# Attention by pairs of heads, and the last layer's expert weights read in rows of 2 and 4 KB

## The chip, the core and the metric

The program runs on one NeuronCore of one Trainium2 chip. TensorE (PE) multiplies matrices into PSUM, VectorE (DVE) and ScalarE (ACT) work on PSUM and SBUF, GpSimd (POOL) copies rows and issues indirect DMAs, and SyncE (SP) issues the transfers of the weights. The metric is the device time of one execution, in microseconds. All numbers are float32; the profile shows each float32 matmul as two PE records, and a transpose as one.

## The reference, cut to what matters

A first block of two layers is followed by a second block of one layer. In the second block the 8 attention heads of width 64 share 2 groups of keys and values, over 512 tokens. Three branches are gated per head and added:

```python
s_cmp = einsum('bghsd,bgcd->bghsc', qh, k_cmp) * scale                  # 31 compressed keys
p_cmp = softmax(where(cmp_mask, s_cmp, -1e30)) * cmp_mask
o_cmp = einsum('bghsc,bgcd->bghsd', p_cmp, v_cmp)
# N_SEL = 16 blocks of 64 cover all 512 tokens: the selected branch is causal attention
s = einsum('bghqd,bgqnld->bghqnl', qb, kg) * scale;  p = softmax(where(ok, s, -1e30))
o_slc = einsum('bghqnl,bgqnld->bghqd', p, vg)
# window 512: the window branch is causal attention with its own keys and values
o_win = einsum('bghnqk,bgnkd->bghnqd', softmax(where(ok_w, s_w, -1e30)), vwb)
o = gates[..., 0:1] * o_cmp + gates[..., 1:2] * o_slc + gates[..., 2:3] * o_win
...
top_i = top_k(where(emask, choice, -inf), 8)[1]        # 8 of 64 experts for each token
swiglu(t_pad[rb], w_gu[e], w_dn[e])                    # w_gu (1024, 512), w_dn (256, 1024)
```

## The kernel before, in words

The program is a list of stages with barriers between them, and each engine's instructions stand in the order in which they are written. Three stages matter.

**Rope** (`rope_stage`, profile from 3691 to 3712 us) rotates queries and keys. Beside it POOL clears `vpad` and copies the values of both causal branches into it (L2228, L2232), each head group's 64 columns with 64 zero columns on either side.

**Attention** (`attention_stage`) takes 96 units: head pair `c2` (4), block `t` of 128 queries (4), head `h` of the pair (2), branch `b` (3: selected, window, compressed). For a unit PE multiplies queries by keys with 64 contraction rows (L2300; L2295 for the compressed branch), adds a mask through the identity (L2302, L2297), later transposes the probabilities in blocks of 128 (L2312) and multiplies by the values (L2329, L2325), whose zero columns put head 0 in PSUM partitions 0 to 63 and head 1 in 64 to 127. DVE takes the maximum (L2348), scales it (L2352), inverts the sum (L2354) and scales the probabilities (L2361). ACT does the exponential with its sum (L2390) and moves the transposed block to SBUF (L2374). PE's order for unit u is scores(u), turn(u-1), values(u-2); DVE finishes unit u before it begins u+1. Score banks are three, banks of transposes two.

**The last layer's experts** (`sparse_experts_stage` with G = 2) hold 64 experts in 32 groups of two. A group's weights are three tiles of 2 MB: gate and up of each expert, and both down matrices. They lie in one of two sets, three slots of the weight ring or `moe_spare`. SP waits until the group before has freed a set (L1362), and before each tile until the tile two before it has landed (L1369), then issues it (L1370). Work goes in units of 64 rows, at least one for each expert, 97 in the profiled execution: POOL copies the gathered rows (L1401) and gathers again (L1386, an indirect DMA of 4 KB rows), PE transposes them (L1415), multiplies gate (L1427) and up (L1429) into PSUM partitions 0 to 63 and 64 to 127, ACT does silu (L1488), DVE the product (L1510), PE a transpose (L1437) and the down product (L1446), DVE copies it out (L1513), and ACT writes it to HBM in two DMAs of 64 rows by 2 KB (L1497). Three waits set the pace of these writes:

```python
act.wait_ge(s.y_copied, u + 2)
act.wait_ge(s.y_out, 32 * u + 64)     # ACT, before it sends unit u: the writes of unit u-1 have landed
...
dve.wait_ge(s.y_out, 32 * u + 32)     # DVE, before it copies unit u: those of unit u-2 have landed
```

Each weight tile lies packed in HBM: a partition's 16 KB are one row. The two layers of the first block use the same function with G = 1.

Of the kernel before, what the change touches and what calls it, by code (L numbers as in the profile page):

```python
# [10 lines left out]
ALU = mybir.AluOpType  # L11
# [5 lines left out]
P = 128  # L17
D = 1024
KD = D // P
T = 512  # L20
# [1298 lines left out]
def sparse_experts_stage(m, tag, first, groups, G, F, hidden, rows, r, source, after):  # L1319
# [25 lines left out]

    with st.block() as block:
        @block.sync
        def _(sp):
            ring.stream(sp, first + 3)
            for j in range(3):  # L1350
                sp.dma_start(bufs[1][j], source(1, j)).then_inc(spare_in[j], 16)
            with sp.Fori(1, halves) as i:
                for half in range(2):
# [3 lines left out]
                    for j in range(3):  # L1357
# [12 lines left out]
                        sp.dma_start(bufs[half][j], source(2 * i + half, j)  # L1370
# [846 lines left out]
def rope_stage(m, p):  # L2217
# [7 lines left out]
    with st.block() as block:  # L2225
        @block.gpsimd
        def _(pool):
# [6 lines left out]
            pool.wait_ge(s.vals, 2 * NT)  # L2234

# [32 lines left out]
def attention_stage(m, p, mT):  # L2268

    nc = m.nc
    st = Stage(m, "attn")
    NB = 3
    pr = st.sb("probs", [P, NB, T])
    pT = st.sb("probsT", [P, 2, NT, P])
    c = st.sb("cols", [P, NB, 4])
    s = st.sem("score top ntop exp total scaled turned t_moved out o_moved masked")

    units = [(c2, t, h, b) for c2 in range(4) for t in range(NT) for h in range(2) for b in range(3)]  # L2280

    def width(u):
        return NC if units[u][3] == 2 else (units[u][1] + 1) * P

    with st.block() as block:
        @block.tensor
        def _(pe):
            def scores(u):
                c2, t, h, b = units[u]
                g, rows, w = c2 // 2, slice(64 * h, 64 * h + 64), width(u)  # L2290
                if u >= 3:
                    pe.wait_ge(s.exp, u - 2)
                ps = m.ps[:, u % 3, :]
                if b == 2:
                    nc.tensor.matmul(ps[:, 0:NC], p.nq[rows, c2, t * P:(t + 1) * P], p.kcmp[rows, g, :],  # L2295
                                     start=True, stop=False)
                    last = nc.tensor.matmul(ps[:, 0:NC], m.ident, mask(p, "cneg")[:, t * NC:(t + 1) * NC],  # L2297
                                            start=False, stop=True)
                else:
                    nc.tensor.matmul(ps[:, 0:w], p.qr[rows, c2, t * P:(t + 1) * P], p.kr[rows, b, g, 0:w],  # L2300
                                     start=True, stop=False)
                    last = nc.tensor.matmul(ps[:, w - P:w], m.ident, mask(p, "causal"), start=False, stop=True)  # L2302
                last.then_inc(s.score, 1)

            def turn(u):
                w = width(u)
# [3 lines left out]
                for j in range(0, w, P):  # L2310
                    n = min(P, w - j)
                    last = nc.tensor.transpose(m.ps[0:n, 3 + u % 2, j:j + P], pr[:, u % NB, j:j + n], m.ident)  # L2312
                last.then_inc(s.turned, 1)

            def values(u):
                c2, t, h, b = units[u]
                g, o = c2 // 2, u // 6
                pe.wait_ge(s.t_moved, u + 1)
                first, final = u % 6 == 0, u % 6 == 5
                if first and o >= 2:  # L2320
                    pe.wait_ge(s.o_moved, o - 1)
# [12 lines left out]
            for u in range(n + 2):  # L2334
                if u < n:
                    scores(u)
                if 1 <= u <= n:
                    turn(u - 1)
# [356 lines left out]
```

## Time and profile before

| | us |
|---|---|
| time before, median of 3 (lowest, highest) | 5263.54 (5261.21, 5282.5) |
| the profiled execution: its own time | 5280.28 |
| its span in the profile | 5278.5 |
| mean granted PE clock, share of full speed | 0.842 |
| attention stage | 3713 to 4001 |
| the last layer's expert stage | 4275 to 5184 |

The page gives, for each engine, the time in which it was busy; the sharing of the span among stages is read from windows. A granted clock of 1.0 is 2.4 GHz and 0.5 is 1.2 GHz. "issue" in a wait means that nothing in the profile is shown as the releaser.

### The profile page before, as it was taken

To read this page: it belongs to the slowest core of one execution; us is meant where nothing else is said; L and a number is where in the kernel's file an instruction comes from. 1 tells how busy PE (TensorE), PEld (TensorE's weight loads), DVE (VectorE), ACT (ScalarE), POOL (GpSimd) and SP (SyncE) were. 2 spreads that over 40 slices of the span, in tenths; PEclk is the share of its full clock that TensorE was granted. 3 is DMA by queue.
4 is the path that set the end of the run, shared out by engine and by line. 5 is a ranking of instruction groups with operands and counts; after the bars stand their busy time and mean duration, and the time that the engine had idled before them with its cause. 6 is when DMAs were issued, how large, how long until landed. Compare 5 with 4: busy or idle time off the path is not lost. (4 is left out here: it accounts for less than half of the span.)

```text
span 5278.5 us, 55308 instructions
## 1 busy us (share of the span) xinstructions
PE 3959.5 (75%) x18979; PEld 2326.6 (44%) x18980; DVE 1353.0 (26%) x2466; ACT 776.8 (15%) x1604; POOL 895.4 (17%) x933
## 2 busy tenths in 40 slices
PE   7699998998387766984888578765998447777772
PEld 3368867983233322433333233323664224444441
DVE  0343453341300012122000120354433301111115
ACT  0232242220011110001111101100221001111110
POOL 0014413430111110001111100321000032222223
PEclk9799999898599988996999889876557679999986
DMA  6470000001399996123999852101001047676685
GB/s 242 121 185 1 1 32 17 1 2 64 115 405 406 386 372 228 48 84 148 393 391 411 337 219 75 54 0 52 7 1 46 33 171 281 248 278 244 252 301 172
DMA packets 144431, 900.30 MB, mean 171 GB/s; under 512 B 52963, under 2 KB 53861, under 8 KB 97829
## 3 DMA queue, kind: packets, MB, share of 16 engines
q1 hardware_dynamic: 95684, 805.05, 40.3%
q0 software_dynamic: 22368, 50.39, 3.0%
q10 hardware_dynamic: 26240, 43.01, 2.5%
q8 instruction: 87, 1.43, 0.1%
q14 instruction: 52, 0.42, 0.0%
HBM read 839.32 MB, written 78.46 MB: 174 GB/s over the span
## 5 line engine op out<-in xcount | busy, mean ns | idle before, releaser
L1427 PE MATMUL ps<-weight_ring,moe_xT 128*64 128x256 f32 (+1 forms) x1344 | 450.1, 490 | 77.9 <-issue 75.7
L1427 PE MATMUL ps<-moe_spare,moe_xT 128*64 128x256 f32 (+1 forms) x1280 | 425.5, 487 | 59.3 <-issue 59.2
L1429 PE MATMUL ps<-weight_ring,moe_xT 128*64 128x256 f32 (+1 forms) x1344 | 450.8, 491 | 0.0
L1429 PE MATMUL ps<-moe_spare,moe_xT 128*64 128x256 f32 (+1 forms) x1280 | 426.2, 488 | 0.0
L1401 POOL COPY moe_xg<-moe_xin 64x1024 f32<-64x1024 f32 x168 | 173.5, 1033 | 1430.5 <-PE ps L1415 802.3
L258 PE MATMUL ps<-weight_ring,mod_wide 128*128 128x512 f32 x640 | 290.7, 609 | 141.8 <-DVE mod_wide L241 132.6
L1510 DVE TENSOR_TENSOR moe_act<-moe_sg,ps 64x256 f32<-64x256 f32 (+1 forms) x164 | 87.2, 532 | 1090.2 <-ACT moe_sg L1488 1090.2
L1427 PEld LDWEIGHTS ps<-weight_ring,moe_xT 128*64 128x64 f32 x1344 | 190.8, 144 | 316.7 <-issue 284.4
L1427 PEld LDWEIGHTS ps<-moe_spare,moe_xT 128*64 128x64 f32 x1280 | 180.3, 143 | 285.8 <-issue 256.3
L1513 DVE COPY moe_y<-ps 128x512 f32 x164 | 113.4, 691 | 714.4 <-PE ps L1446 577.0
L1446 PE MATMUL ps<-weight_ring,moe_aT 128*64 128x512 f32 x944 | 256.5, 680 | 15.7 <-issue 15.6
L1446 PE MATMUL ps<-moe_spare,moe_aT 128*64 128x512 f32 x904 | 248.4, 687 | 14.3 <-issue 14.3
L258 PEld LDWEIGHTS ps<-weight_ring,mod_wide 128*128 128x128 f32 x640 | 121.4, 194 | 310.0 <-issue 176.0
L1437 PE MATMUL ps<-base,moe_act 64*128 64x64 f32 x462 | 61.7, 239 | 249.4 <-DVE moe_act L1510 249.4
L1312 POOL DMA_INDIRECT slot_table<-disp_ids,moe_dest x48 | 47.0, 979 | 1080.5 <-DVE moe_dest L1297 1067.1
L1488 ACT ACTIVATE moe_sg<-ps 64x256 f32<-64x256 f32 (+1 forms) x164 | 75.8, 462 | 1019.0 <-PE ps L1429 674.5
L1429 PEld LDWEIGHTS ps<-weight_ring,moe_xT 128*64 128x64 f32 x1344 | 190.6, 144 | 0.0
L1386 POOL DMA_INDIRECT moe_xin<-hidden,moe_icol x174 | 166.1, 955 | 137.3 <-POOL moe_icol L1382 135.7
L1415 PE MATMUL ps<-base,moe_xg 64*128 64x64 f32 x1336 | 151.2, 237 | 47.1 <-POOL moe_xg L1401 47.1
L1429 PEld LDWEIGHTS ps<-moe_spare,moe_xT 128*64 128x64 f32 x1280 | 180.3, 143 | 0.0
L1720 PE MATMUL ps<-hT,weight_ring 128*128 128x512 f32 x384 | 168.9, 603 | 9.9 <-DMA weight_ring<-in_w_in_b_dram 8.0
L527 PE MATMUL ps<-delta_hx,weight_ring 128*128 128x512 f32 x384 | 171.7, 602 | 5.6 <-PEq L184 5.6
(508 smaller groups left out, 6254.4 us busy)
## 6 DMA issues: line engine op xcount, KB each, us to landing
weight_ring<-in_w_dram SPq DMA_DIRECT2D x96, 2048.0 KB, 10.8
moe_spare<-in_w_dram SPq DMA_DIRECT2D x96, 2048.0 KB, 10.7
weight_ring<-in_w_exp_gu_dram SPq DMA_DIRECT2D x32, 2048.0 KB, 9.8
moe_spare<-in_w_exp_gu_dram SPq DMA_DIRECT2D x32, 2048.0 KB, 14.7
weight_ring<-in_ada_w_dram SPq DMA_DIRECT2D x24, 2048.0 KB, 8.1
expert_rows<-moe_y ACTq DMA_DIRECT2D x328, 128.0 KB
weight_ring<-in_w_exp_dn_dram SPq DMA_DIRECT2D x16, 2048.0 KB, 11.6
moe_spare<-in_w_exp_dn_dram SPq DMA_DIRECT2D x16, 2048.0 KB, 11.2
```

The costliest lines, as they stand in the source:

```text
L258: last = nc.tensor.matmul(m.ps[:, u % 4, :], wide[:, v, k, :], w[:, k, :], start=(k == 0), stop=(k == KD - 1))
L527: last = nc.tensor.matmul(m.ps[:, b, :], w[:, k, h * P:(h + 1) * P], hx[:, k, CT:CT + T], start=(k == 0), stop=(k == KD - 1))
L1386: nc.gpsimd.indirect_dma_start(out=xin[:, b, :], out_offset=None, in_=hidden, in_offset=bass.IndirectOffsetOnAxis(ap=icol[:, b:b + 1], axi ...
L1401: nc.gpsimd.tensor_copy(xg[:], xin[:, b, :]).then_inc(s.x_moved, 1)
L1415: last = nc.tensor.transpose(m.ps[:, 2, k * UR:(k + 1) * UR], xg[:, k * P:(k + 1) * P], m.ident[0:UR, 0:UR])
L1427: nc.tensor.matmul(m.ps[0:UR, 0, 0:F], xT[:, k, :], gate[:, k, :], start=(k == 0), stop=(k == KD - 1))
L1429: last = nc.tensor.matmul(m.ps[UR:P, 0, 0:F], xT[:, k, :], up[:, k, :], start=(k == 0), stop=(k == KD - 1))
L1446: last = nc.tensor.matmul(m.ps[h * UR:(h + 1) * UR, 5, :], aT[:, j, :], down[:, j, h * 512:(h + 1) * 512], start=(j == 0), stop=(j == FC - 1))
L1488: nc.scalar.activation(sg[UR:P, :], m.ps[0:UR, 0, 0:F], ACT.Silu).then_inc(s.silu, 1)
L1510: nc.vector.tensor_tensor(act_[:], sg[UR:P, :], m.ps[UR:P, 0, 0:F], ALU.mult).then_inc(s.act, 1)
L1513: nc.vector.tensor_copy(yo[:, bass.ds((u % 2) * 512, 512)], m.ps[:, 5, :]).then_inc(s.y_copied, 1)
L1720: last = nc.tensor.matmul(m.ps[:, 4 * (c % 2) + j, :], w[:, k, q * P:(q + 1) * P], hT[:, k, :], start=(k == 0), stop=(k == KD - 1))
```

## The change

Attention has 36 units: for each head pair one unit of the compressed branch over all 512 queries, then four blocks of queries for each causal branch. A unit holds both heads. Their scores stand next to each other in the program, head 0 on contraction rows 0 to 63 into one bank, head 1 on rows 64 to 127 into the next. The values are multiplied once per branch and head pair, for all queries that see a block of keys (512, 384, 256 and 128 columns), each head with 64 output columns into its own half of the PSUM partitions; `vpad`, its clearing and its copies are gone, and `vs` and `vw` are read in place. PE's order is scores(u), turn(u-2), values(u-3); there are two pairs of score banks and one pair of banks for the transposes. DVE does top(u) and then scale(u-1). ACT moves both heads in one instruction, and copies out 512 queries at once.

The last layer's expert weights are no longer packed: the gate and up tile is read as 8 rows of 2 KB per partition, 256 KB apart in HBM, and the down tile as 4 rows of 4 KB, 512 KB apart. They land in the same places in SBUF.

```diff
@@ sparse_experts_stage
+    def landing(j):
+        return packed(SLOT) if G == 1 else shape(j)
...
-                sp.dma_start(bufs[1][j], source(1, j)).then_inc(spare_in[j], 16)
+                sp.dma_start(landing(j)(bufs[1][j]), source(1, j)).then_inc(spare_in[j], 16)
...
-                        sp.dma_start(bufs[half][j], source(2 * i + half, j)
+                        sp.dma_start(landing(j)(bufs[half][j]), source(2 * i + half, j)
@@ rope_stage
-            nc.gpsimd.memset(p.vpad[:], 0.0).then_inc(s.zeroed, 1)
-            pool.wait_ge(s.zeroed, 1)
-            for i, v in enumerate((p.vs, p.vw)):
-                for t in range(NT):
-                    nc.gpsimd.tensor_copy(p.vpad[:, i, t, :, 64:128],
-                                          v[:, t, :].rearrange("p (g d) -> p g d", g=2)).then_inc(s.vals, 1)
@@ attention_stage
-    units = [(c2, t, h, b) for c2 in range(4) for t in range(NT) for h in range(2) for b in range(3)]
+    units = [(c2, k, t) for c2 in range(4) for k in range(3) for t in (range(NT) if k else [NT - 1])]
...
-                if u >= 3:
-                    pe.wait_ge(s.exp, u - 2)
+                if u >= 2:
+                    pe.wait_ge(s.exp, 2 * (u - 1))
...
-                    nc.tensor.matmul(ps[:, 0:w], p.qr[rows, c2, t * P:(t + 1) * P], p.kr[rows, b, g, 0:w],
-                                     start=True, stop=False)
-                    last = nc.tensor.matmul(ps[:, w - P:w], m.ident, mask(p, "causal"), start=False, stop=True)
+                    for h in range(2):
+                        nc.tensor.matmul(ps[:, h, 0:w], p.qr[half[h], c2, t * P:(t + 1) * P],
+                                         p.kr[half[h], k - 1, g, 0:w], start=True, stop=False)
+                    for h in range(2):
+                        last = nc.tensor.matmul(ps[:, h, w - P:w], m.ident, mask(p, "causal"), start=False, stop=True)
...
-                pe.wait_ge(s.scaled, u + 1)
-                if u >= 2:
-                    pe.wait_ge(s.t_moved, u - 1)
+                pe.wait_ge(s.scaled, 2 * u + 2)
+                if u >= 1:
+                    pe.wait_ge(s.moved, u)
...
-                    for j in range(t + 1):
-                        last = nc.tensor.matmul(ps, p.vpad[:, b, j, g, lo:lo + P], pT[:, u % 2, j, :],
-                                                start=(first and j == 0), stop=final)
+                    for j in range(NT):
+                        for h in range(2):
+                            last = nc.tensor.matmul(m.ps[64 * h:64 * h + 64, o, j * P:T], v[:, j, 64 * g:64 * g + 64],
+                                                    pT[:, k - 1, h, j, j * P:T], start=False,
+                                                    stop=(k == 2 and j == NT - 1))
@@ plan_weights, and source(g, j) of the last layer alike
-            ring.add([(packed(SLOT), a["w_exp_gu_2"][2 * e + j])])
-        ring.add([(packed(SLOT), a["w_exp_dn_2"][e])])
+            ring.add([(whole(KD, 512), a["w_exp_gu_2"][0, 2 * e + j].rearrange("(k p) n -> p k n", p=P))])
+        ring.add([(whole(4, D), a["w_exp_dn_2"][0, 2 * e:2 * e + 2].rearrange("o (k p) n -> p (o k) n", p=P))])
```

How the order changes at three places. First PE in the middle of a head pair, before: single heads, blocks of 256 and 384 keys (`mix_kr` the keys, `mix_qr` the queries, `attn_probs` a transpose, `attn_probsT` with `mix_vpad` the values).

```order
L2300 MATMUL ps<-mix_kr,mix_qr 128x256
L2302 MATMUL ps<-mix_masks,base 128x128
L2312 MATMUL ps<-base,attn_probs 31x128
L2329 MATMUL ps<-attn_probsT,mix_vpad 128x128 x2
L2300 MATMUL ps<-mix_kr,mix_qr 128x256
L2302 MATMUL ps<-mix_masks,base 128x128
L2312 MATMUL ps<-base,attn_probs 128x128 x2
L2325 MATMUL ps<-attn_probsT,mix_vpadc 128x128
L2295 MATMUL ps<-mix_kcmp,mix_nq 128x31
```

And PE now, at the end of a branch: both heads' scores, the transposes of the unit two before, and the values of the whole branch.

```order
L2303 MATMUL ps<-mix_kr,mix_qr 128x256 x2
L2306 MATMUL ps<-mix_masks,base 128x128 x2
L2318 MATMUL ps<-base,attn_probs 128x128 x8
L2303 MATMUL ps<-mix_kr,mix_qr 128x384 x2
L2306 MATMUL ps<-mix_masks,base 128x128 x2
L2318 MATMUL ps<-base,attn_probs 128x128 x2
L2335 MATMUL ps<-attn_probsT,mix_vs 64x512 x2
L2335 MATMUL ps<-attn_probsT,mix_vs 64x384 x2
L2335 MATMUL ps<-attn_probsT,mix_vs 64x256 x2
L2335 MATMUL ps<-attn_probsT,mix_vs 64x128 x2
```

The value products have moved from every unit to the end of a branch, and are 8 for a head pair and branch where they were 20; between two groups of scores there is now one pair of masks and a run of transposes.

Second DVE, now, inside a causal branch: the maximum of the next unit (`attn_cols<-ps`) stands before the inverse of the sum and the two scalings of the unit before it, where it stood behind them.

```order
L2364 TENSOR_REDUCE attn_cols<-ps 128x2
L2365 TENSOR_SCALAR attn_cols<-attn_cols 128x2
L2383 RECIPROCAL attn_cols<-attn_cols 128x2
L2386 TENSOR_SCALAR attn_probs<-attn_probs,attn_cols,mix_ng 128x384 x2
L2364 TENSOR_REDUCE attn_cols<-ps 128x2
L2365 TENSOR_SCALAR attn_cols<-attn_cols 128x2
L2383 RECIPROCAL attn_cols<-attn_cols 128x2
L2386 TENSOR_SCALAR attn_probs<-attn_probs,attn_cols,mix_ng 128x512 x2
```

Each row serves two heads, so that the row counts of the stage's reduces fall from 96 to 40.

Third SP in the loop of the last layer's experts, now; before, the three transfers stood at the same places with the shape 128x4096.

```order
L1373 ISA
L1373 DMA weight_ring<-in_w_exp_gu_dram 128x8x512
L1373 ISA
L1373 DMA weight_ring<-in_w_exp_gu_dram 128x8x512
L1369 REGISTER_ALU
L1373 ISA
L1373 DMA weight_ring<-in_w_exp_dn_dram 128x4x1024
```

Nothing has moved there; only the shape of the transfers differs.

## Rows read from the trace of the kernel before

**Rows 1.** Windows, attention and experts: busy of each engine, PEclk, DMA share, GB/s.

```profile
3713.00:4001.00 288.00, 281.51 (x957) 196.84 (x956) 111.25 (x416) 81.42 (x304) 0.00 (x0) 0.56 0.00 1
4275.00:5184.00 909.00, 688.86 (x4856) 413.57 (x4854) 108.09 (x194) 119.77 (x292) 210.77 (x292) 0.91 0.70 255
```

**Rows 2.** The same, 58 us inside one head pair.

```profile
3792.00:3850.00 58.00, 57.81 (x178) 39.58 (x178) 21.69 (x79) 15.45 (x57) 0.00 (x0) 0.50 0.00 1
```

**Rows 3.** Timeline of PE in attention: start, length, records (xN), idle before.

```profile
3971.80 0.79 PE L2325 MATMUL ps<-attn_probsT,mix_vpadc 31*128 31x128 f32 x2
3972.52 0.63 PE L2295 MATMUL ps<-mix_kcmp,mix_nq 64*128 64x31 f32 x2
3973.08 0.63 PE L2297 MATMUL ps<-mix_masks,base 128*128 128x31 f32 x2
...
3975.62 2.07 PE L2300 MATMUL ps<-mix_kr,mix_qr 64*128 64x512 f32 x2
3977.62 0.79 PE L2302 MATMUL ps<-mix_masks,base 128*128 128x128 f32 x2
...
3978.42 1.49 PE L2329 MATMUL ps<-attn_probsT,mix_vpad 128*128 128x128 f32 x6
```

**Rows 4.** Groups by form, DVE and ACT in attention: count, busy, mean ns.

```profile
L2390 ACT ACTIVATE attn_probs<-ps,attn_cols 128x512 f32<-128x512 f32 x16 | 11.0, 687 | 60.9 <-DVE attn_cols L2352 60.9
...
L2348 DVE TENSOR_REDUCE attn_cols<-ps 128x1 f32<-128x512 f32 x16 | 11.1, 691 | 39.9 <-PE ps L2302 39.9
...
L2348 DVE TENSOR_REDUCE attn_cols<-ps 128x1 f32<-128x128 f32 x16 | 4.6, 290 | 16.0 <-PE ps L2302 15.9
```

**Rows 5.** Timeline of PE in the experts: gate and up in two column halves.

```profile
4559.63 0.38 PE L1427 MATMUL ps<-weight_ring,moe_xT 128*64 128x256 f32 x1
4559.67 0.38 PE L1429 MATMUL ps<-weight_ring,moe_xT 128*64 128x256 f32 x1
4559.85 0.38 PE L1427 MATMUL ps<-weight_ring,moe_xT 128*64 128x256 f32 x1
```

**Rows 6.** Timelines of ACT and SP in the experts.

```profile
4359.78 1.12 SPq L1370 DMA_DIRECT2D weight_ring<-in_w_exp_gu_dram  x2
4360.77 1.28 ACTq L1497 DMA_DIRECT2D expert_rows<-moe_y  x2
...
4374.10 1.28 ACTq L1497 DMA_DIRECT2D expert_rows<-moe_y  x2
...
5154.72 0.38 ACT L1488 ACTIVATE moe_sg<-ps 64x256 f32<-64x256 f32 x1 [6.31 <-PE ps L1429]
...
5163.09 0.38 ACT L1488 ACTIVATE moe_sg<-ps 64x256 f32<-64x256 f32 x1 [6.21 <-PE ps L1429]
...
5170.22 0.38 ACT L1488 ACTIVATE moe_sg<-ps 64x256 f32<-64x256 f32 x1 [4.96 <-PE ps L1429]
```

**Rows 7.** Windows from issue to issue (SP): ACT L1488 alone, its count is units.

```profile
4331.29:4359.78 28.49, 1.13 (x3) 0.94 0.72 262
4468.22:4489.10 20.88, 0.75 (x2) 0.84 0.90 344
4515.80:4550.53 34.73, 1.50 (x4) 0.95 0.62 227
```

**Rows 8.** Waits in the expert stage: total us, times, longest.

```profile
DVE moe_y L1513 <- DMA expert_rows<-moe_y: 127.2, 30, 5.0
SPq L1362 <- PE ps L1446: 550.6, 30, 40.3
```

**Rows 9.** DMA from 4360 to 4375: packets, MB, share of 16 engines.

```profile
q1 hardware_dynamic: 315, 4.64, 84.8%
q10 hardware_dynamic: 160, 0.26, 5.2%
```

**Rows 10.** The same, 8 us each: 2 MB of 4 KB and of 16 KB rows.

```profile
q1 hardware_dynamic: 528, 2.10, 73.7%
q1 hardware_dynamic: 144, 2.10, 73.5%
```

More of the change, by code:

```diff
@@ L2303, in scores @@
                 last.then_inc(s.score, 1)
             def turn(u):
-                w = width(u)
-                pe.wait_ge(s.scaled, u + 1)
-                if u >= 2:
-                    pe.wait_ge(s.t_moved, u - 1)
-                for j in range(0, w, P):
-                    n = min(P, w - j)
-                    last = nc.tensor.transpose(m.ps[0:n, 3 + u % 2, j:j + P], pr[:, u % NB, j:j + n], m.ident)
+                _, k, t = units[u]
+                pe.wait_ge(s.scaled, 2 * u + 2)
@@ L2313, in turn @@
+                if u >= 1:
+                    pe.wait_ge(s.moved, u)
+                for h in range(2):
+                    for j in range(t + 1):
+                        rows, src = (NC, pr[:, u % NB, h, j * NC:(j + 1) * NC]) if k == 0 else \
+                                    (P, pr[:, u % NB, h, j * P:(j + 1) * P])
+                        last = nc.tensor.transpose(m.ps[0:rows, 4 + h, j * P:(j + 1) * P], src, m.ident)
                 last.then_inc(s.turned, 1)
             def values(u):
-                c2, t, h, b = units[u]
@@ L2317, in values @@
[L2317 to L2321, printed above, removed]
-                ps = m.ps[:, 6 + o % 2, 0:P]
-                lo = 64 if h == 0 else 0
-                if b == 2:
-                    last = nc.tensor.matmul(ps, p.vpad_c[:, g, lo:lo + P], pT[0:NC, u % 2, 0, :],
-                                            start=first, stop=final)
-                else:
-                    for j in range(t + 1):
-                        last = nc.tensor.matmul(ps, p.vpad[:, b, j, g, lo:lo + P], pT[:, u % 2, j, :],
-                                                start=(first and j == 0), stop=final)
+                c2, k, _ = units[u]
@@ L2331, in values @@
                 last.then_inc(s.out, 1)
-            n = len(units)
-            for u in range(n + 2):
+            for u in range(n + 3):
                 if u < n:
                     scores(u)
-                if 1 <= u <= n:
-                    turn(u - 1)
-                if u >= 2:
-                    values(u - 2)
+                if 2 <= u < n + 2:
+                    turn(u - 2)
+                if u >= 3 and units[u - 3][2] == NT - 1:
+                    values(u - 3)
         @block.vector
@@ L2364, in _, with exp @@
+            for u in range(n + 1):
+                if u < n:
+                    top(u)
+                if u >= 1:
+                    scale(u - 1)
         @block.scalar
         def _(act):
+            def exp(u):
+                _, k, t = units[u]
+                act.wait_ge(s.ntop, u + 1)
+                if k == 0:
+                    e = pr[:, u % NB, :, 0:CW]
+                    nc.scalar.activation(e, e, ACT.Exp, scale=0.125).then_inc(s.exp, 2)
+                    return
+                if u >= NB:
+                    act.wait_ge(s.turned, u - NB + 1)
+                w = (t + 1) * P
+                for h in range(2):
+                    nc.scalar.activation(pr[:, u % NB, h, 0:w], blocks(u)[:, h, 0:w], ACT.Exp,
+                                         bias=c[:, u % 4, 1, h:h + 1], scale=0.125,
+                                         accum_out=c[:, u % 4, 2, h:h + 1]).then_inc(s.exp, 1)
@@ L2396, in attention_stage @@
+            for u in range(n + 4):
+                if u < n:
+                    exp(u)
+                if 2 <= u < n + 2:
+                    move(u - 2)
+                if u >= 4 and units[u - 4][1:] == (2, NT - 1):
+                    out(units[u - 4][0])
     st.close()
```

151 lines of the change are left out of this document (84 added, 67 removed).

## The prediction

> **What bounds the kernel now.** I read the windows of the two stages first, then in attention the timeline of PE, in the experts the timelines of ACT and SP, and last the waits and the DMA shares.
>
> Attention takes 288 us and PE is busy in 281.5 of them, DVE in 111, ACT in 81 [rows 1]. It is bound by PE, and the reader should see at which clock: the mean granted clock is 0.56, and 0.50 through 58 us in which PE is busy in 57.8 [rows 2]. So PE works almost without a gap at 1.2 GHz.
>
> The expert stage takes 909 us, with PE busy in 689 and the DMA engines at a share of 0.70 [rows 1]. Neither is full. SP waits 550.6 us in 30 waits for PE to free a set of weights [rows 8], so on the whole the weights are early. What is late are the small writes. At 4359.78 SP issues the next weights; at 4360.77 ACT issues the writes of a unit; it issues the next ones only at 4374.10, 13.3 us later [rows 6]. Where no weights are loading, silu follows silu 7.13 us apart (5163.09 to 5170.22), and 8.37 where an expert changes (5154.72 to 5163.09) [rows 6]. The wait for landed writes, on DVE alone, comes to 127.2 us in 30 waits [rows 8], 30 being also the number of groups that SP loads in the loop.
>
> **Attention, term by term, at 1.2 GHz.** Six value records take 1.49 us with 0.42 for the last, so one record of 128 columns takes 0.214 and one product (two records) 0.43 [rows 3]. A transpose is one record, 0.214. A wide score takes 2.00 us from its start to that of the mask, against 4 x 0.43 = 1.71, so 0.29 goes to the change to 64 rows and back [rows 3]. A compressed unit costs 0.72 for values, 0.56 for scores [rows 3], and I take 0.5 for its mask.
>
> Before: scores 160 blocks of 128 keys x 0.43 = 68; masks 64 x 0.43 = 27; changes 64 x 0.29 = 19; transposes (160 + 32) x 0.214 = 41; values 160 x 0.43 = 68; compressed 32 x 1.78 = 57. Sum 280, against 288 measured.
>
> After:
> - scores: if the two heads' products on different rows run together, 80 x 0.43 = 34. No row of before shows two row halves at work. Bounds: 68, as now, and 34. Column halves are shown: gate and up records start 0.04 us apart, and the next gate record 0.22 us after the first (4559.63, 4559.67, 4559.85), what one alone of 256 columns needs at 2.4 GHz, 2 x 0.107 [rows 3, 5]. I take 34, the row of the nearest kind.
> - values: 20480 columns for both heads before; now column halves, so 80 x 0.43 = 34, and 8 changes x 0.29 = 2. This pair is of the kind that the row shows.
> - masks 27, transposes 41, as before; changes 36 x 0.29 = 10.
> - compressed: values 4 x 2.0 = 8, scores 16 pairs x 0.56 = 9 (18 if not together), masks 8 x 0.43 = 3.
>
> Sum 168, or 211 if rows don't pair. To this come PE's waits. Two turns of the loop hold one chain: top (reduce of 1024 columns, by the line through 0.290 for 128 and 0.691 for 512 [rows 4]: 1.23, and 0.15 for the scaling), two exponentials of 0.69 + 0.09 (1.56), the move of 1024 columns (about 1.0), 8 transposes (1.7), the next scores and masks (2.85): 8.5 us for two units of the widest kind, against PE's own 2 x (2.85 + 1.7) = 9.1. PE stays the bound at 1.2 GHz, with little margin; I add 13 us for the start of each branch and the narrow units. That is 181 us. At 2.4 GHz the chain of two widest units falls to 1.4 + 1.56 + 1.0 + 0.85 + 1.4 = 6.2, 3.1 a unit, and with 1.5, 2.0 and 2.6 for the narrower ones a branch takes 9.2 us, the compressed unit about 4 and unhidden values 6: 4 x (18.4 + 10) = 114, say 120. The clock therefore leaves 120 to 181. The stage keeps PE busy with the same kinds of work at the same low clock; I take 170, near the slow end, because the clock now is 0.56 and not 0.50 [rows 1, 2]. **Gain 118**, bounds 77 - 13 = 64 (rows not paired, low clock) and 168.
>
> One price for row halves is only stated: the Trainium skill ("TensorE: Matmul & The Clock Gate", "Measured speedup vs the span model") gives the span of packed tiles as one product plus about 4 ns per further tile. No run here shows it yet; with it the term would be the 34 above.
>
> The cleared `vpad` I cost at nothing: POOL's clearing and copies stand beside the rotation on PE and DVE, and attention waits for both. Fewer instructions on DVE and ACT gain nothing either; both idle more than half of the stage.
>
> **The experts, term by term.** From issue to issue of SP a group takes 20.88 us with 2 units, 28.49 with 3, 34.73 with 4 [rows 7]. Undisturbed units would give 7.13 (n - 2) + 8.37 + 8.8, the two long ones for the two experts: 17.2, 24.3, 31.4. The difference is 3.7, 4.2 and 3.3, near 4 us per group, and it is the one long stop of a write behind the weights. In a load window the q1 packets take 0.848 x 16 x 15 / 315 = 0.65 us each; the write queue q10 has 160, of which 128 carry 2 KB, and 0.052 x 240 / 128 = 0.10 us each [rows 9]. A write puts 8 packets on each engine; if each waits for one weight packet of 16 KB that is 8 x 0.75 = 6 us and more, if for one of 2 KB, 8 x 0.2 = 1.6. The rest of the 13.3 us is what is already ahead in the engines. So with short rows the writes should land within 5 us, under the 7.13 that a unit lasts, and neither ACT nor DVE waits. The gathers of 4 KB rows are served sooner too, but POOL has two units of time for them.
>
> What the short rows cost: 2 MB in rows of 4 KB held the engines for 73.7% of 8 us, in rows of 16 KB for 73.5% [rows 10]: nothing. For 2 KB the bounds are this and the q10 packet, 0.10 us for 2 KB, against 0.65 / 8 = 0.08 for 2 KB of a long row: 20% more. A group's 6.3 MB hold the engines 15.5 to 19 us, 20 with the other traffic. So a group of 2 units no longer ends at 17.2 but near 20. Of the 29 intervals between SP's issues, 8 are of 2 units (21.2 on the mean), 13 of 3 (28.3), 7 of 4 (35.6), one of 5 (42.2): 8 x 1.2 + 13 x 4.0 + 7 x 4.1 + 3.7 = 94, with the 30th **98 us**. Bounds from the same count: 120 if loads cost nothing more, 87 if they take 21 us.
>
> **Sum.** 118 + 98 = 216 from the profiled execution, 5280.3, is 5064. That execution lies 17 us above the median of the runs shown, near the slowest; from the median it would be 5048. I give 5050.
>
> **Rivals.**
> - *The writes stay as late* (chance 0.14). If the engines change queues only after about 16 KB, whatever the rows, the writes wait as now. For it: the 13.3 us are long against 8 alternations. Against it: nothing in the rows shows grouping. Then only attention gains, and 2-unit groups lose a few us: 5160. The Trainium skill says so in "DMA: Bandwidth & Descriptors", "Queues, rings and completion order": an engine drains a whole packet of some 9 to 17 descriptors from one ring before it turns to the next. No row of before decides it.
> - *Row halves don't run together* (0.08). Scores and compressed scores cost 43 us more: 5095.
> - *The clock rises in attention* (0.12). PE gets longer runs of wide products, and at the ends of head pairs its clock already rises now and then (0.56 on the mean against 0.50 inside a pair [rows 1, 2]). Then the chain over DVE and ACT is the bound, 120 to 135: 5005.
> - *The loads become the bound, and the kernel is slower* (0.04). 1024 short reads 256 KB apart could run at half the rate. The point from which this decides is 32.5 us per group: then 8 groups lose 11.3, 13 lose 4.2 and 8 still gain 3.7, +116 in all, as much as attention gains. At 36 us (175 GB/s) it is +217 x 30/29: 5385. Against it: 4 KB rows 512 KB apart, which cost nothing [rows 10].
> - Both parts as forecast: 0.62.
>
> **The numbers.** The likeliest case alone spans 5010 to 5100 (attention 155 to 185 us, experts 80 to 115 gained). The range 4990 to 5165 takes in the fast clock, the unpaired rows and the late writes. What can be told from no change is about 0.5%, 26 us: faster than that 0.94, within it 0.02, slower 0.04.
>
> **What would show it.** In attention: L2303 records of two heads starting within 0.1 us of each other; L2335 pairs likewise; the stage 155 to 185 us long with PE still busy above 85%. If PE's share is under 75% the chain bounds it. In the experts: gaps between ACT's writes no longer than 9 us at an issue of weights, L1516's wait for the DMA near zero, SP intervals of 20, 24 to 25 and 31 to 32 us for 2, 3 and 4 units, q1 packets near 0.09 us. I am wrong if the intervals stay at 28 and 35 us, or if SP's waits for PE vanish and its waits for landed tiles grow.

## The result, and the profile after

The changed kernel takes 4974.22 us (median of 4 runs, 4966.88 to 4977.01) against 5266.51 us (median of 4, 5261.21 to 5282.5). The ratio is 0.9438, 95% interval 0.9415 to 0.9461, a gain of 292 us. The profiled execution took 4974.38 us, its span is 4972.6 us (before 5278.5). The prediction, 5050 us with a range of 4990 to 5165, had the direction right and was too high.

The span lost 305.9 us. I took the start of the same product in both traces as marks: 12.4 us lie ahead of the rotation and the attention, 157.5 in these two, 2.9 between them and the experts, 133.1 from the first product of the experts to the end.

The windows of the two stages after the change (as in [rows 1]):

```profile
3699.80:3832.60 132.80, 110.42 (x673) 69.45 (x673) 68.77 (x188) 63.80 (x173) 0.00 (x0) 0.88 0.00 1
4102.00:4878.00 776.00, 637.85 (x4857) 394.90 (x4856) 107.78 (x194) 119.06 (x292) 210.78 (x292) 0.98 0.87 301
```

Attention went from 288 us to 133, and the mean granted clock from 0.56 to 0.88. PE was busy for 98% of the stage and is now for 83%. The waits in attention say who waits for whom (total us, times, longest):

```profile
ACT attn_probs L2408 <- DVE attn_cols L2365: 52.2, 27, 3.9
DVE attn_cols L2364 <- PE ps L2306: 47.3, 26, 3.5
...
PE ps L2318 <- ACT attn_probsT L2421: 18.9, 14, 3.1
```

No engine is full; the exponentials wait for the maxima, these for the scores, and PE's transposes for ACT's moves of the unit before. The lines of the score products and of the value products, each in a window of some 3 us (count, then shortest, median and longest in ns):

```profile
L2303 PE MATMUL ps<-mix_kr,mix_qr x4: 589/641/693, 3754.1 to 3754.6; 64*128 64x512 f32 x4
...
L2335 PE MATMUL ps<-attn_probsT,mix_vs x16: 272/432/643, 3751.8 to 3753.9; 128*64 128x512 f32 x4, 128*64 128x384 f32 x4, 128*64 128x256 f32 x4, 128*64 128x128 f32 x4
```

The timeline of PE over the same stretch groups them:

```profile
3751.46 0.41 PE L2318 MATMUL ps<-base,attn_probs 128*128 128x128 f32 x2 [0.68 <-ACT attn_probsT L2421]
3751.80 2.37 PE L2335 MATMUL ps<-attn_probsT,mix_vs 128*64 128x512 f32 x16
3754.10 1.13 PE L2303 MATMUL ps<-mix_kr,mix_qr 64*128 64x512 f32 x4
```

Four score records of 0.64 us lie within 1.13 us, so the row halves of two heads run together; before, one head's product took 2.07 us at half the clock [rows 3]. Sixteen value records, 7.0 us in sum, lie within 2.37.

In the experts the timeline of ACT shows the units (L1491 is silu, L1500 the writes):

```profile
4146.52 0.38 ACT L1491 ACTIVATE moe_sg<-ps 64x256 f32<-64x256 f32 x1 [4.96 <-PE ps L1432]
...
4151.94 1.43 ACTq L1500 DMA_DIRECT2D expert_rows<-moe_y  x2
4155.31 0.38 ACT L1491 ACTIVATE moe_sg<-ps 64x256 f32<-64x256 f32 x1 [6.62 <-PE ps L1432]
...
4160.42 1.19 ACTq L1500 DMA_DIRECT2D expert_rows<-moe_y  x2
4162.43 0.38 ACT L1491 ACTIVATE moe_sg<-ps 64x256 f32<-64x256 f32 x1 [4.96 <-PE ps L1432]
...
4167.48 1.19 ACTq L1500 DMA_DIRECT2D expert_rows<-moe_y  x2
4169.55 0.38 ACT L1491 ACTIVATE moe_sg<-ps 64x256 f32<-64x256 f32 x1 [4.96 <-PE ps L1432]
...
4177.95 0.38 ACT L1491 ACTIVATE moe_sg<-ps 64x256 f32<-64x256 f32 x1 [6.23 <-PE ps L1432]
```

SP issued weights at 4150.51, and the writes of the next unit still follow 8.5 us later, where it took 13.3 before [rows 6]. Of the 96 distances between writes in this stage 30 were over 10 us before, one for each group, and 8 are now. A group of three units is 7.12 + 7.12 + 8.40 (or 8.79): one long step, not two. The windows from issue to issue, silu alone (as in [rows 7]):

```profile
4127.98:4150.51 22.53, 1.12 (x3) 1.00 0.93 330
4242.57:4260.87 18.30, 0.75 (x2) 1.00 0.96 328
4302.94:4333.50 30.56, 1.50 (x4) 1.00 0.80 274
```

The waits of the stage, and the DMA over 15 us of a load (the kind of [rows 8] and [rows 9]):

```profile
DVE moe_y L1516 <- DMA expert_rows<-moe_y: 184.3, 60, 3.1
ACT moe_sg L1491 <- DMA expert_rows<-moe_y: 16.1, 3, 6.2
...
SPq L1365 <- PE ps L1449: 332.8, 30, 31.4
```

```profile
q1 hardware_dynamic: 1931, 3.92, 78.1%
q10 hardware_dynamic: 295, 0.50, 9.7%
```

A weight packet costs 0.781 x 16 x 15 / 1931 = 0.097 us, before 0.65. DVE's wait for landed writes grew from 127.2 us in 30 waits to 184.3 in 60, while the stage got 133 us shorter. It stands ahead of DVE's wait for PE's down product, and that one fell from 220.8 us to 140.0: what the first takes more is time that DVE would have spent on the second. The wait of ACT for a write ahead of silu tells the cost better: 81.6 us in 13 before, 16.1 in 3 now.

### The profile page after: what moved, and what is told of

It is laid out like the page before. It is cut to its first block and busy times, and to the rows that moved or that the text cites. A ratio compares the mean times of both kernels' runs of the same rounds, so it can differ in the third digit from the quotient of the medians.

```text
span 4972.6 us, 54079 instructions
## 1 busy us (share of the span) xinstructions
PE 3731.7 (75%) x18691; PEld 2178.1 (44%) x18692; DVE 1310.5 (26%) x2238; ACT 757.4 (15%) x1472; POOL 887.8 (18%) x924
## 5 line engine op out<-in xcount | busy, mean ns | idle before, releaser
L1430 PE MATMUL ps<-weight_ring,moe_xT 128*64 128x256 f32 (+1 forms) x1344 | 444.9, 486 | 71.3 <-issue 69.0
L1432 PE MATMUL ps<-weight_ring,moe_xT 128*64 128x256 f32 (+1 forms) x1344 | 445.9, 487 | 0.0
L1516 DVE COPY moe_y<-ps 128x512 f32 x164 | 113.4, 691 | 690.5 <-PE ps L1449 495.8
L1449 PE MATMUL ps<-weight_ring,moe_aT 128*64 128x512 f32 x944 | 241.1, 645 | 26.7 <-issue 16.6
L1449 PE MATMUL ps<-moe_spare,moe_aT 128*64 128x512 f32 x904 | 227.0, 636 | 23.6 <-issue 16.1
L1491 ACT ACTIVATE moe_sg<-ps 64x256 f32<-64x256 f32 (+1 forms) x164 | 75.8, 462 | 888.4 <-PE ps L1432 872.3
L1418 PEld LDWEIGHTS ps<-base,moe_xg 64*128 64x128 f32 x1336 | 109.2, 140 | 136.8 <-issue 136.8
```

What stands on the lines that cost most here:

```text
L1418: last = nc.tensor.transpose(m.ps[:, 2, k * UR:(k + 1) * UR], xg[:, k * P:(k + 1) * P], m.ident[0:UR, 0:UR])
L1430: nc.tensor.matmul(m.ps[0:UR, 0, 0:F], xT[:, k, :], gate[:, k, :], start=(k == 0), stop=(k == KD - 1))
L1432: last = nc.tensor.matmul(m.ps[UR:P, 0, 0:F], xT[:, k, :], up[:, k, :], start=(k == 0), stop=(k == KD - 1))
L1449: last = nc.tensor.matmul(m.ps[h * UR:(h + 1) * UR, 5, :], aT[:, j, :], down[:, j, h * 512:(h + 1) * 512], start=(j == 0), stop=(j == FC - 1))
L1491: nc.scalar.activation(sg[UR:P, :], m.ps[0:UR, 0, 0:F], ACT.Silu).then_inc(s.silu, 1)
L1516: nc.vector.tensor_copy(yo[:, bass.ds((u % 2) * 512, 512)], m.ps[:, 5, :]).then_inc(s.y_copied, 1)
```

## The experiments

Theory A for attention: each head's scores over its own 64 rows, alone, hold the granted clock down; pairs or full rows let it rise. The rival T1: the clock falls when PE works without gaps. For the experts, theory A: a row of a write waits at each of its turns for one weight packet, so the landing falls with the length of the weights' rows. The rival, B: the loads themselves became better. The runs e3 to e10, e12 and e13 are one execution each; the four of the change span 10 us.

**Each part alone.** `e1_attention_alone`: the change with the weights packed as before.

```diff
-                sp.dma_start(landing(j)(bufs[1][j]), source(1, j)).then_inc(spare_in[j], 16)
+                sp.dma_start(bufs[1][j], source(1, j)).then_inc(spare_in[j], 16)
```

> The changed attention with the experts' weights packed in rows of 16 KB as before. If the two parts add, this run shows the attention part alone: the stage from the first score to the first projection product lasts 131 us as in the changed kernel, and the whole is near 5266 - 158 = 5108 us. The expert stage then takes 909 us from first to last unit as before, and groups of 2, 3 and 4 units 21, 28 and 35.5 us. The rival (the shorter attention also changed the state of the DMA or of the clock for the experts) expects an expert stage shorter by 10 us or more without the short rows.

`e2_short_rows_alone`: the change with the attention and rotation functions of before.

> The attention and rope stages of before, with the short rows of the change. If the parts add: attention 289 us at a granted clock near 0.56, experts about 776 us with groups of 18, 23.5 and 30 us, the whole near 5266 - 133 = 5133 us. The rival: the two parts share something, and this run gains clearly less or more than 133.

Measured: 5143.85 us (ratio 0.9748, interval 0.9731 to 0.9764) and 5133.7 us (0.9725, 0.9709 to 0.9741), before 5277.9 on that chip. The parts gain 134 and 144 us, 278 together, near the whole. The first is 36 us above its forecast of 5108: attention alone took 133 us for the stage, a gain of 157, but the expert stage came out 20 to 25 us longer than in the trace of before, with the same code: intervals of 21.6, 29.6 and 36.5 us for 2, 3 and 4 units against 21.2, 28.3 and 35.6. Why the same write stops cost more there stays open.

**What sets the clock.** `e3_scores_apart` computes each head's scores and its mask before the other's, so no row halves run together:

```diff
                     for h in range(2):
                         nc.tensor.matmul(ps[:, h, 0:w], ..., start=True, stop=False)
-                    for h in range(2):
                         last = nc.tensor.matmul(ps[:, h, w - P:w], m.ident, mask(p, "causal"), ...)
```

> The changed kernel, but each head's causal mask product stands right behind its scores, so that the two row halves cannot run together; nothing else. Theory A (the paired row halves raised the clock): the granted clock of attention falls from 0.88 to about 0.56 and the stage grows from 131 to 200 us or more. Theory B (the clock comes from the wide value products, or simply from the new order): the clock stays above 0.8 and the stage grows by the unpaired products alone, 80 blocks x 0.21 = 17 us less what hides in waits, 140 to 150 us.

`e4_values_in_128` cuts the value products into 128 columns each, two heads still side by side:

```diff
-                            last = nc.tensor.matmul(m.ps[64 * h:64 * h + 64, o, j * P:T], ...
+                        for x in range(j, NT):
+                            for h in range(2):
+                                last = nc.tensor.matmul(m.ps[64 * h:64 * h + 64, o, x * P:(x + 1) * P], ...
```

> The changed kernel, with the values multiplied in products of 128 columns (160 for both causal branches and two heads' halves side by side, where 64 wider ones stand); the columns and the column halves stay. Theory B1 (the long value products raised the clock): the clock of attention falls towards 0.56, the stage grows to 170 us or more. Theory A (packing of the array): the clock stays above 0.8 and the stage within 5 us of 131.

`e8_values_over_128_rows` takes the value products of one head after the other over all 128 output columns:

```diff
-                            last = nc.tensor.matmul(m.ps[64 * h:64 * h + 64, o, j * P:T], v[:, j, 64 * g:64 * g + 64],
+                            lo = 64 if h == 0 else 0
+                            last = nc.tensor.matmul(m.ps[:, o, j * P:T], p.vpad[:, k - 1, j, P * g + lo:P * g + lo + P],
```

> The change, but the value products of the two heads go over all 128 output columns (values padded with zeros on the other head's side), one head behind the other, and not as two column halves side by side; the scores stay in pairs of row halves. Per pair of heads the value products then take 16 rows of 512 and fewer columns one after the other, some 9,000 to 10,000 columns in place of half of that. Theory A (it is two products side by side that keep the granted clock at 1.00, whichever halves they use): the clock falls to 0.5 for part of each pair and attention grows from 133 us to 170 to 190 us, near the run in which the scores were apart (183 us). Theory B (the chain over DVE and ACT bounds attention, and TensorE's clock is high whenever TensorE has work with gaps in it): value products at 2.4 GHz add about 2 us per pair, at most 16 us in all, 135 to 150 us.

`e9_scores_three_times`:

```diff
+                    for again in range(3):
                         for h in range(2):
-                            nc.tensor.matmul(ps[:, h, 0:w], ..., start=True, stop=False)
+                            nc.tensor.matmul(ps[:, h, 0:w], ..., start=True, stop=again < 2)
```

> The change, but each pair of score products of the two sliding and selected parts is issued three times (the last one counts; the output stays the same), always in row halves side by side. It fills TensorE, which was busy for 110 of 133 us, with paired work: 20 more pairs per pair of heads, by the 1.13 us of a pair of 64x512 some 35 us more in all. Theory T1 (the granted clock falls when TensorE works without gaps, and it was high only because TensorE waited for ACT and DVE): the clock goes to 0.5 for long stretches as before the change, attention takes 200 us or more. Theory T2 (it falls when products use half of the 128 rows and stand alone, and stays high for pairs and full products however busy TensorE is): the clock stays at 0.85 to 1.00, attention takes 145 to 160 us.

`e10_scores_over_128_rows`, and the same edit in the attention of before, `e13_old_attention_over_128_rows`, which is otherwise e2 (the rotation stage, not shown, clears the other head's rows of the keys):

```diff
-                        nc.tensor.matmul(ps[:, h, 0:w], p.qr[half[h], c2, t * P:(t + 1) * P],
-                                         p.kr[half[h], k - 1, g, 0:w], start=True, stop=False)
+                        nc.tensor.matmul(ps[:, h, 0:w], p.qr[:, c2, t * P:(t + 1) * P],
+                                         p.kr[:, k - 1, g, h, 0:w], start=True, stop=False)
```

> The change, but the scores of the two heads follow each other, each over all 128 rows (keys padded with zeros in the other head's 64 rows), so that no two run side by side and none uses half of the rows alone; columns of work as in the run with the scores apart (183 us, granted clock 0.75 in the mean). Theory T2 (half-filled rows lower the clock): the clock stays high, 0.85 or more, and attention takes what paired scores took plus the work of the other half at 2.4 GHz, 17 us at most: 140 to 152 us. Theory T1 (busy without gaps lowers it, whatever the rows): as with the scores apart, 175 to 190 us.

> The attention of before the change (one head and one query tile at a time, no product beside another), with the short rows of the change in the experts; the one edit is that the score products of the selected and sliding parts go over all 128 rows (keys padded with zeros in the other head's rows). The products, their count and their columns stay the same; with half-filled rows this attention took 287 to 290 us, TensorE busy for 280 of them, at a mean granted clock of 0.57. Theory T2 (a stretch of products of which many use half of the rows alone lowers the clock, and this alone held attention at 1.2 GHz before): the mean clock rises to 0.85 or more, TensorE's work shrinks to 280 x 0.57 / 0.9 = 177 us, attention takes 180 to 215 us (the chain over DVE and ACT then shows), the whole about 5050 us (e2 had 5134). Theory T3 (the clock before was low for another reason, the transposes and the 128-column products of one tile at a time, so that padding changes nothing): 285 to 290 us, 5134 us.

Measured: the windows of attention in e3, e4, e8, e9, e10 and e13, in this order (length, PE, PEld, DVE, ACT, POOL, clock, DMA share, GB/s).

```profile
3700.10:3882.80 182.70, 166.06 (x672) 93.38 (x672) 68.98 (x188) 63.99 (x173) 0.00 (x0) 0.75 0.00 1
```

```profile
3705.70:3840.70 135.00, 114.50 (x864) 83.59 (x864) 68.98 (x188) 64.12 (x173) 0.00 (x0) 0.85 0.00 1
```

```profile
3704.00:3855.90 151.90, 130.18 (x673) 85.67 (x673) 68.72 (x188) 64.52 (x177) 0.00 (x0) 0.90 0.00 1
```

```profile
3703.00:3863.10 160.10, 142.16 (x929) 91.33 (x929) 68.73 (x188) 63.89 (x173) 0.00 (x0) 0.91 0.00 1
```

```profile
3703.10:3838.50 135.40, 111.92 (x673) 77.48 (x673) 68.94 (x188) 64.63 (x177) 0.00 (x0) 0.94 0.00 1
```

```profile
3716.00:3919.00 203.00, 170.39 (x960) 134.62 (x960) 106.90 (x416) 84.32 (x308) 0.00 (x0) 0.92 0.00 1
```

In e3 the scores apart cost 50 us and the clock falls to 0.75, the way theory A had it but only part of the way (it gave 0.56 and 200 us). Long value products are not what keeps it up (e4), nor are the column halves: with values one head after the other it is 0.90, and the 19 us more go with 20 us more of busy PE for the doubled columns (e8, above the 150 us that theory B gave). With the paired scores issued three times PE is busy for 142 of 160 us, fuller than the 110 of 133 of the change, and the clock is 0.91. e10, with full rows one after the other, has 0.94 and 135.4 us, below the 140 to 152 us that were expected. e3 and e10 have the same number of records, 672 and 673, none beside another in the scores, 64 rows in one and 128 in the other, and 183 us against 135; but the masks stand in another place too.

The clean pair is e2 and e13, which differ in the rows of the scores alone (and in what prepares the keys ahead of the stage). e2, its whole attention:

```profile
3716.80:4006.90 290.10, 282.61 (x960) 197.61 (x961) 111.33 (x416) 82.39 (x305) 0.00 (x0) 0.56 0.00 1
```

From first to last product that is 290 us against 201.5 in e13, and the clock goes from 0.56 to 0.92; the kernel took 5064.42 us, e2 without it 5133.7 (the traced execution of e2, 5151.1, is the slowest of its four). T1 falls by this pair, and also by a stretch of the trace of before in which PE works without any gap on products over all 128 rows (L1720):

```profile
2140.00:2200.00 60.00, 60.00 (x141) 26.60 (x140) 10.03 (x15) 1.79 (x3) 0.00 (x0) 1.00 0.00 0
```

A wide score product in the timeline of e13:

```profile
3760.71 1.02 PE L2308 MATMUL ps<-mix_kr,mix_qr 128*128 128x512 f32 x2
```

Twice the rows, half of the 2.07 us of [rows 3]. What held the clock low before is thus shown: the score products over half of the rows, alone. The stage still hangs on PE: e8 and e9 keep it busy for 20 and 32 us more than the change does, and are 19 and 27 us longer.

**Rows of the weights and the write.** `e5_rows_8k`, `e6_rows_4k` and `e12_rows_1k` land all three tiles in rows of 8, 4 and 1 KB, laid out so in HBM (n is 2, 4 and 16; the edit of e5):

```diff
-        return packed(SLOT) if G == 1 else shape(j)
+        if G == 1:
+            return packed(SLOT)
+        n = 2 if j == 2 else 2
+        return whole(n, SLOT // n)
```

> The change as it is, but all three tiles of an expert in the last layer come in rows of 8 KB (two of a partition) in place of 2 KB. Theory A: a row of a unit's output waits at each of its turns for one packet of the weights, so its landing falls with the length of the weight rows (about 11 us with 16 KB rows, 6.3 us with 2 KB rows, about 4 us of that a first delay that stays); with 8 KB rows it should take some 7 us, just about one unit of 7.13 us, so that part of the groups still stall: intervals of about 20, 26 and 33 us at 2, 3 and 4 units, between the 21.6, 29.6 and 36.5 us of the run with 16 KB rows and the 18.1, 23.5 and 30.3 us of the change, and a time of 5010 to 5070 us. Theory B: only the packed form of 16 KB held the writes back, and any shorter row gives all of it: 4975 us, intervals as in the change.

> The same with rows of 4 KB, the length in which the loop before the change loaded the down weights of the other layers. Theory A (landing falls with row length, and only its part above one unit of 7.13 us costs anything): landing at about 6 to 7 us, intervals at 3 and 4 units within 1 us of the change's 23.5 and 30.3 us, time 4970 to 5000 us. A rival, that 2 KB is needed because the cost is proportional to the row length: a quarter of the way from the change (4974 us) to the long rows (5144 us), some 5000 to 5020 us.

> The change with the tiles of the last layer in rows of 1 KB. Theory A (a part of the write's landing is per turn of a weight packet, the rest is a first delay of about 4 us that does not depend on it): intervals at 3 and 4 units as with 2 KB, 23.5 and 30.3 us, and 4970 to 4985 us. A rival: packets this small cost more than they carry; the 2 KB packet took 84 ns, and if a 1 KB packet takes 60 ns or more the load of an expert of 6 MB needs 22 us in place of 15 or less, so that all groups of 2 and 3 units become bound by their loads: 5100 us or more.

`e7_half_the_writes` keeps rows of 16 KB and leaves out the second half of the columns of the last layer's expert output:

```diff
+    H = 1 if G == 2 else 2
...
-                for h in range(2):
+                for h in range(H):
                     act.dma_start(rows[bass.ds(u * UR, UR), h * 512:(h + 1) * 512], ...
```

> Long rows of 16 KB as before the change, attention as changed; each unit of the last layer writes only the first half of its output columns, so that one write in place of two is issued per unit and each DMA engine has 4 rows of it in place of 8 (the output of that layer is left out for the second half of the columns). Theory A (rows of the writes take turns with long weight packets of 0.61 us): the write needs about 4 + 4 x 0.7 = 7 us after its issue in place of 11, most of the stall goes with the weights still in long rows: intervals of about 19, 25 and 32 us at 2, 3 and 4 units, 5000 to 5050 us. Theory B (it is the weight loads themselves that got shorter or earlier with short rows, and the writes have little to do with it): intervals stay at 21.5, 29.5 and 36.5 us, 5130 to 5144 us.

Measured. Intervals are means from issue to issue of SP; landing is the median, over the writes in whose first 6 us the weight packets fill more than half of the engines, from issue to the end of the last record of a write's packets; all worked out from the records of the traces.

| rows | landing us | 2 units | 3 units | 4 units | time us |
|---|---|---|---|---|---|
| 16 KB (e1) | 9.2 | 21.6 | 29.6 | 36.5 | 5143.85 |
| 8 KB (e5) | 8.0 | 17.3 | 26.8 | 33.9 | 5034.89 |
| 16 KB, half the write (e7) | 7.5 | 16.9 | 25.4 | 32.6 | 5011.59 |
| 4 KB (e6) | 6.6 | 17.2 | 23.5 | 30.6 | 4976.95 |
| 2 KB gate/up, 4 KB down (the change) | 6.3 | 18.1 | 23.5 | 30.3 | 4974.22 |
| 1 KB (e12) | 6.0 | 19.2 | 23.6 | 29.9 | 4985.40 |

The 9.2 of e1 stands between two kinds: of 60 writes some 30 land after about 7 us, and the other 30, those issued right behind a load's start, after about 11.5 (11.0 before the change); these are the stops. With rows of 8 KB none takes 9 us.

Theory A holds in order and in rough size: the time follows the landing, also where the weights stay long and only the write is halved (e7), which B had at 5130 us or more. At 7.5 us (e7) the landing still costs, at 6.6 and below it costs nothing more, with one unit of 7.13 us in between. The turns themselves can be read in the records of the trace of before. In its expert stage 5150 packets of the writes end while at least eight weight packets are under way. For 62% of them a weight packet starts exactly 4 ns before the recorded end, for 8% one of the gathers, for 6% another write packet; at any other nanosecond near by it is 2 to 3% for the weights. So after one row of a write most engines turn to the weights again. What A had wrong is 2 units with rows of 8 KB: 17.3 and not 20. Both rivals of the short rows fall: no cost in proportion to length between 4 and 2 KB, and no bound by loads at 1 KB except for groups of 2 units, which lose 1.1 us each. The 1 KB packets, from the DMA view over 160 us of the stage:

```profile
q1 hardware_dynamic: 40394, 41.04, 81.7%
```

That is 0.817 x 16 x 160 / 40394 = 0.052 us each, 19.8 GB/s for one engine against 21 with 2 KB.

**A version beyond the change.** `e11_rows_4k_moves_by_head` combines rows of 4 KB with moves of each head's transposed probabilities by themselves:

```diff
-                pe.wait_ge(s.scaled, 2 * u + 2)
-                if u >= 1:
-                    pe.wait_ge(s.moved, u)
                 for h in range(2):
+                    pe.wait_ge(s.scaled, 2 * u + 1 + h)
+                    if u >= 1:
+                        pe.wait_ge(s.moved, 2 * u - 1 + h)
```

> A version that may beat the change: all expert tiles of the last layer in rows of 4 KB (that run took 4977.0 us against the 4974.2 us median of the change), and in attention each head's transposed probabilities move out of their bank by themselves, so that TensorE's transposes of the next unit wait for one head's move and not for both. The wait of TensorE for these moves was 18.9 us in 14 waits; half of it at most is saved, and ACT gains 26 more instructions of some 0.2 us fixed cost each. Expected: attention 125 to 133 us, total 4965 to 4977 us, 0 to 0.2 per cent faster than the change, which would be near the bound of what can be told. If ACT was the later engine instead, 135 us or more and slower than the change.

Its median is 4969.23 us (5 runs, 4962.14 to 4971.02), ratio 0.9417 (0.9397 to 0.9436). The interval overlaps that of the change, so in the whole it can't be told from it. The stage itself shows the step, in its window and its wait:

```profile
3709.00:3835.50 126.50, 107.76 (x673) 68.15 (x673) 68.73 (x188) 65.60 (x209) 0.00 (x0) 0.91 0.00 1
```

```profile
PE ps L2321 <- ACT attn_probsT L2425: 15.1, 13, 2.9
```

126.5 us, where the six traces with the attention of the change as it is (the change, e1, e5, e6, e7, e12) have 132.7 to 134.6; the wait itself fell only from 18.9 to 15.1.

## Why the prediction was right or wrong

**PE bounds attention at 1.2 GHz: right for before, wrong as a forecast.** The step that failed is "the stage keeps PE busy with the same kinds of work at the same low clock; I take 170". The kinds of work were not the same: the scores now run as pairs over 128 rows, and e3, e10 and above all e13 show that the clock goes with this: 0.56 with the scores alone over 64 rows, 0.92 with the same scores over 128. The value was 133 us, inside the two ends that the working gave (120 to 181) and near the fast one, the gain 157 in place of 118. The rival "the clock rises" had the chance 0.12 and a stage of 120 to 135 us: right in size. Its bound, the chain over DVE and ACT, was right only in part: PE is busy for 83% and not under 75, and work added to PE came back almost whole in the stage (e8, e9). Its reason ("longer runs of wide products") was wrong: cut to 128 columns they left the clock at 0.85 (e4). Of the 157 us some 88 come with full rows and the clock alone, by e13 against e2; the other 69, fewer and wider products and the new order, were not told apart.

**Row halves run together: right** (four records of 0.64 us in 1.13). But with e10's full rows in turn the stage takes 135.4 us; running together saved 2.6 us beyond what full rows give, in one execution each.

**The stop of a write behind long packets: right**, shown by the row lengths, by e7 and by the turns of single packets. The rival "the writes stay as late" falls: no write of the change lands later than 9 us, where half of those into a load took 9 to 12 before. The prediction said that the Trainium skill says the same as this rival. What the page ("DMA: Bandwidth & Descriptors", "Queues, rings and completion order") gives is a turn of some 9 to 17 descriptors, not one of 16 KB. As an estimate from it, with a descriptor for each row, a write would first wait 9 x 0.65 = 5.9 us or more beside rows of 16 KB and 9 x 0.097 = 0.9 us beside 2 KB, so a shorter landing with shorter rows doesn't speak against the page. The turns do: with 8 rows of a write on each engine taken in one turn, one write packet in eight would be followed by a weight packet, and 62% are. For these writes the measurement decides against the page. "Land within 5 us" was too low: 6.3, still under a unit. It took all that stands ahead of a write to shrink with the rows, and the first delay of about 4 us doesn't.

**The size of the experts' gain, 98 us: measured 133.** The mis-sized term is the floor of a group, 7.13 (n - 2) + 8.37 + 8.8. The trace after has one long step per group, 8.4 or 8.8 in turn, so the floor is 7.13 (n - 1) + 8.6: 15.7, 22.9 and 30.0 in place of 17.2, 24.3 and 31.4. I had read 8.37 and 8.8 as two steps of one group where they belong to groups in alternating buffers. 1.4 us x 30 groups is 42 us, and 35 more than forecast came in; groups of 2 units end at 18.1 and not at their floor of 15.7 (forecast 20), which with rows of 1 KB becomes 19.2: their loads hold them. The bound of 120 that the prediction gave used the same floor and was no bound.

**"L1516's wait for the DMA near zero": wrong.** It grew to 184.3 us, while undisturbed units stayed at 7.12 us. The intervals came, near the forecast 20, 24 to 25 and 31 to 32 us and each 1 to 2 us less, and so did packets of 0.097 us and score records of two heads 7 ns apart. "No gap over 9 us between writes at an issue of weights" came in part: 15 are left where 30 were, the longest 13.2 us. Of the two signs of being wrong that go together, SP's wait for PE fell to 332.8 us but is not gone, and its waits for landed tiles grew, from 238.5 us to 317.9: the loads are nearer to being the bound than before.

**The rest.** 12.4 us came ahead of the changed stages. At the last product before the rotation the eleven other kernels with the new attention lie 2.9 to 16.2 us ahead of the trace of before, the two others with the old attention 4.6 and 5.1 us behind. No instruction there was changed; the cause is open. 216 forecast, 306 in the span: 39 from attention, 35 from the experts, 15 from here and between. The 14 us taken off because the profiled execution lies above the median were right: the spans differ by 306 us, the medians by 292. So the median was missed by 76 us. Either error alone, 39 or 35 us, would have left the time inside the range; both fell to the same side.

## What to carry to other kernels

When PE is busy all the time and the granted clock is near 0.5, look at how many rows its products use before counting columns: padding the keys with zeros to 128 rows took 88 us off the stage, more than half of the 157 us that rewriting it gave. A small write that must land within one step of a loop should not share the engines with long rows; here 4 KB was short enough, and at 1 KB only the groups of 2 units lost, 1.1 us each. The total of a wait in the list is not its cost: read by how much the distance between two passes of the same line grows.

## What the runs showed of the hardware

- In attention the granted clock went with the rows in use and not with how busy PE is: in the mean 0.56 at 97% busy with lone 64-row scores (e2), 0.92 at 84% with the same scores over 128 rows (e13), 0.91 at 89% with pairs issued three times (e9); and 1.00, the level of 2.4 GHz, through 60 us of the trace of before in which PE is busy for 60.0 on products over 128 rows.
- Unpaired full-row scores cost almost no more time than paired halves (135.4 against 132.8 us), with PE busy for 111.9 and 110.4 us and the clock at 0.94 and 0.88.
- Rows of a write and rows of a load took turns one by one: in the trace of before 62% of the write packets that end under a load hand over to a weight packet, 6% to another write packet.
- Part of a write's landing does not depend on the weights' rows: into a load, the first of its packets starts about 4 us after the issue with rows of 16 KB and of 2 KB alike, and 1.2 us with idle queues. No run looked for the cause.
